# Router of a mixture of experts on unscaled rows, partly inside the product before it

## The reference

```python
def rms_norm(x, g):
    xf = x.astype(jnp.float32)
    y = xf * lax.rsqrt(jnp.mean(xf * xf, axis=-1, keepdims=True) + RMS_EPS)
    return (y * g.astype(jnp.float32)).astype(x.dtype)
...
    g_logits = (xf @ w_rg).astype(jnp.float32) + b_rg.astype(jnp.float32)      # 4 groups
    g_prob = jax.nn.softmax(g_logits, axis=-1)
    g_idx = jnp.argmax(g_logits, axis=-1)
    g_gate = jnp.take_along_axis(g_prob, g_idx[:, None], axis=1)[:, 0]
    e_logits = ...                                                             # 8 experts of that group
    top_vals, top_idx = lax.top_k(e_logits, MOE_TOPK)                          # top 2
    e_gate = jax.nn.softmax(top_vals, axis=-1) * g_gate[:, None]
    ...
    hdn = jax.nn.silu(xb @ w_gate[e]) * (xb @ w_up[e]); return hdn @ w_down[e]
```

## Time and profile before

| | |
|---|---|
| median of 3 runs | 1922.25 us (1921.8 to 1922.73) |
| the profiled execution | 1922.67 us, span 1920.6 us, mean granted TensorE clock 0.968 |
| busy, share of the span | TensorE 91%, VectorE 37%, ScalarE 34%, GpSimd 35% |
| HBM read | 525.82 MB, 274 GB/s over the span |

### The profile page before, as it was taken

How to read it: one execution, slowest core, us unless ns; L and a number is a source line. 1 busy time by engine, 2 the same in 40 slices (tenths; PEclk the granted TensorE clock), 3 DMA queues, 4 the chain that set the end, 5 groups by cost and what they waited for, 6 DMA issues and landing times.

```text
span 1920.6 us, 27786 instructions
## 1 busy us (share of the span) xinstructions
PE 1749.7 (91%) x9070; PEld 1094.1 (57%) x9070; DVE 710.0 (37%) x1363; ACT 656.6 (34%) x1318; POOL 666.4 (35%) x536
## 2 busy tenths in 40 slices
PE   6999999998799999998769999999987999999997
PEld 5889766787444343343358897667864433443432
DVE  5528576423321221221255285674232212222211
ACT  4565555754111111111145665557441111111110
POOL 6688655796000000000056886557950000000000
PEclk9999899998899999999989998999988999999999
DMA  6444211455699999999924442114557999999995
GB/s 254 169 176 174 91 45 45 176 221 218 279 421 426 428 427 428 428 428 427 395 97 158 176 176 89 45 45 176 233 205 291 427 428 427 427 429 427 428 427 251
DMA packets 39770, 528.87 MB, mean 275 GB/s; under 512 B 4248, under 2 KB 7064, under 8 KB 7872
## 3 DMA queue, kind: packets, MB, share of 16 engines
q1 hardware_dynamic: 39584, 526.89, 66.7%
q0 software_dynamic: 32, 0.02, 0.0%
HBM read 525.82 MB, written 1.06 MB: 274 GB/s over the span
## 4 chain that ended last, share of the span: by engine, by line
PE 49%; issue 32%; POOL 8%; DMA 5%; DVE 4%; ACT 1%; SPq 0%; POOLq 0%; DVEq 0%; ACTq 0%
PE PS L1038 9%; POOL view L1946 8%; PE PS L721 5%; PE PS L723 5%; PE PS L722 5%; PE PS L1069 5%; DMA view<-in_w_exp_up_dram 5%; PE PS L855 2%; PE PS L815 2%; PE PS L816 2%; PE PS L817 2%; DVE view L1588 2%; PE PS L1019 2%; PE PS L890 1%; PE PS L1004 1%
## 5 line engine op out<-in xcount | busy, mean ns | idle before, releaser
L1946 POOL TENSOR_TENSOR view<-view,view 128x512 fp32r<-128x512 f32 x448 | 578.6, 1314 | 650.1 <-ACT view L1158 645.3
L1038 PE MATMUL PS<-view,view 128*64 128x512 f32 x2048 | 447.7, 593 | 26.7 <-DMA view<-in_w_exp_up_dram 18.1
L1158 ACT ACTIVATE view<-view 128x512 fp32r<-128x512 f32 x448 | 273.6, 628 | 201.0 <-PE PS L723 189.8
L1038 PEld LDWEIGHTS PS<-view,view 128*64 128x64 f32 x2048 | 146.8, 137 | 321.5 <-issue 321.4
L721 PE MATMUL PS<-view,view 128*128 128x512 f32 x704 | 296.3, 421 | 8.9 <-POOL view L1946 7.2
L723 PE MATMUL PS<-view,view 128*128 128x512 f32 x704 | 276.0, 392 | 0.0
L722 PE MATMUL PS<-view,view 128*128 128x512 f32 x704 | 275.8, 392 | 0.0
L1069 PE MATMUL PS<-view,view 128*64 128x512 f32 x1024 | 231.9, 606 | 1.0 <-ACT view L1407 1.0
L1839 DVE TENSOR_TENSOR view<-PS,view 128x512 f32<-128x512 f32 x32 | 22.1, 692 | 486.7 <-PE PS L1019 421.3
L721 PEld LDWEIGHTS PS<-view,view 128*128 128x128 f32 x704 | 133.6, 190 | 47.4 <-POOL view L1946 12.6
L722 PEld LDWEIGHTS PS<-view,view 128*128 128x128 f32 x704 | 133.6, 190 | 32.8 <-issue 8.2
(11 more groups left out here) (241 smaller groups left out, 2055.8 us busy)
## 6 DMA issues: line engine op xcount, KB each, us to landing
view<-in_w_exp_gate_dram SPq DMA_DIRECT2D x64, 2048.0 KB, 19.9
view<-in_w_exp_up_dram SPq DMA_DIRECT2D x64, 2048.0 KB, 22.7
view<-in_w_exp_down_dram SPq DMA_DIRECT2D x64, 2048.0 KB, 25.8
view<-in_w_mix_dram SPq DMA_DIRECT2D x56, 2048.0 KB, 8.0
view<-bias_table SPq DMA_DIRECT2D x2, 1536.0 KB, 11.4
view<-in_x_dram SPq DMA_DIRECT2D x1, 1024.0 KB, 5.2
out_dram<-view SPq DMA_DIRECT2D x1, 1024.0 KB, 5.3
dtw<-in_w_dt_dram SPq DMA_DIRECT2D x2, 256.0 KB, 11.0
```

The lines of the kernel that those rows point to most:

```text
L1038: ins = pe.matmul(bank(ph, name, j)[e * CAP:(e + 1) * CAP, :], xgT2[h % 2][:, k, at + e * CAP:at + (e + 1) * CAP], slot8[expert_block(j, k ...
L1158: nc.scalar.activation(highs(chunk), weights(slot8, chunk), ACT.Copy).then_inc(*high_ready.up(ph))
L1946: g_.tensor_tensor(weights(low8, chunk), weights(slot8, chunk), highs(chunk), ALU.subtract).then_inc(*low_ready.up(ph))
```

## The change

The transposes and the logits work on `X` itself, before the row factor 1/sqrt is known; the factor (one number for each token) is applied where the bias is added. So the transposes of `X` for blocks 0 to 3 and the logits of blocks 0 to 3 are put behind chunks of the product `("wo", 1)`. The logits are now made transposed, 36 rows by 256 tokens in 8 f32 products (`lgT`), copied out by ScalarE, and turned back by two small products with the identity. `XNh` is made from `X` with the factor as scale (ScalarE), `XNl` by VectorE instead of GpSimd. Mask, `tris` and `ones` for the ranks are bf16. The gate exponentials and the gates move behind the selection of the first four experts, and ranks count from 1 (`iota` starts at 1), which drops one operation. The last two early weight loads wait for `lgT` instead of `lg`.

```diff
-                sp.wait_ge(*full(ph, "lg"))
+                sp.wait_ge(*full(ph, "lgT"))
...
-                product(ph, both("wo", 1), FB + 12, 1, mgTh, mgTl)
-
-                pe.wait_ge(*xn_ready.at(ph, 4))
-                for k in range(KD):
-                    transpose2(ph, lambda t: XN[:, t, k * P:(k + 1) * P], ("h2", k))
-                for k in range(KD - 2, KD):
+                def row_transposes(k):
+
+                    for t in range(TT):
+                        pe.wait_ge(*out_of(ph, "wo", k // 4, t))
+                    transpose2(ph, lambda t: X[:, t, k * P:(k + 1) * P], ("h2", k))
+
+                def logits(k):
+
+                    if k == 0:
+                        pe.wait_ge(*free(ph, "lgT"))
                     pe.wait_ge(*out_of(ph, "h2", k))
+                    return pe.matmul(bank(ph, "lgT")[0:36, 0:TT * P], wr[:, k, :], hT[:, k, :],
+                                     start=(k == 0), stop=(k == KD - 1))
+
+                def first_rows(k):
+
+                    if 1 <= k <= 4:
+                        row_transposes(k - 1)
+                    elif k in (5, 6):
+                        for i in (2 * (k - 5), 2 * (k - 5) + 1):
+                            logits(i)
+
+                product(ph, both("wo", 1), FB + 12, 1, mgTh, mgTl, behind=first_rows)
+                for k in range(KD // 2, KD):
+                    row_transposes(k)
+                for k in range(KD // 2, KD):
+                    ins = logits(k)
+                ins.then_inc(*fill(ph, "lgT"))
+                pe.wait_ge(*out_of(ph, "lgT"))
                 pe.wait_ge(*free(ph, "lg"))
                 for t in range(TT):
-                    for k in range(KD):
-                        ins = pe.matmul(PS[:, 0, t * 36:(t + 1) * 36], hT[:, k, t * P:(t + 1) * P], wr[:, k, :],
-                                        start=(k == 0), stop=(k == KD - 1))
+                    ins = pe.matmul(PS[:, 0, t * 36:(t + 1) * 36], lgs[:, t * P:(t + 1) * P], ident[0:36, 0:36],
+                                    start=True, stop=True)
...
                         act.wait_ge(*out_of(ph, "wo", n, t))
+                        nc.scalar.activation(sq[:, (2 * n + t) * COLS:(2 * n + t + 1) * COLS],
+                                             X[:, t, n * COLS:(n + 1) * COLS], ACT.Square,
+                                             accum_out=small[:, 2 * n + t:2 * n + t + 1]).then_inc(*sumsq.up(ph))
+                    for k in ((4, 6, 7) if n else (0, 2)):
+                        scaled(ph, hT[:, k, :], ("h2", k), G2 + k)
+                act.wait_ge(*full(ph, "lgT"))
+                nc.scalar.activation(lgs, bank(ph, "lgT")[0:36, 0:TT * P], ACT.Copy).then_inc(*drain(ph, "lgT"))
+                act.wait_ge(*r_ready.at(ph, 1))
+                act.wait_ge(*sumsq.made(ph))
                 for t in range(TT):
...
+                    ins = nc.scalar.activation(XNh[:, t, :], X[:, t, :], ACT.Copy, scale=st[:, 64 + t:65 + t])
+                ins.then_inc(*xnh_ready.up(ph))
...
-                norm_rows(8, 15, 4)
-                for k in range(1, KD, 2):
-                    scaled(hT[:, k, :], ("h2", k), G2 + k)
-
+                    for k in ((5,) if n else (1, 3)):
+                        scaled(hT[:, k, :], ("h2", k), G2 + k)
+                dve.wait_ge(*sumsq.at(ph, 17))
+                link(v.tensor_tensor(st[:, 0:TT], small[:, 0:TT], small[:, TT:2 * TT], ALU.add))
+                r_row = rsqrt(TT, 8, D, r_ready)
...
+                for t in range(TT):
+                    ins = v.scalar_tensor_tensor(out=logit[:, t, :], in0=PS[:, 0, t * 36:(t + 1) * 36],
+                                                 scalar=r_row[:, t:t + 1], in1=bc_rb, op0=ALU.mult, op1=ALU.add)
+                ins.then_inc(*drain(ph, "lg"))
...
+                link(v.scalar_tensor_tensor(out=rt[:, 3], in0=rt[:, 2], scalar=-3.0 * BIG, in1=l32,
+                                            op0=ALU.mult, op1=ALU.add))
                 first_max(rt[:, 3], v2, rt[:, 4], rt[:, 5], EXPERTS)
...
+                v.tensor_tensor(maskh[:, :, :], rt[:, 2], rt[:, 5], ALU.add).then_inc(*mask_ready.up(ph))
+                dve.wait_ge(*xnh_ready.at(ph, 1))
+                for t in range(TT):
+                    ins = v.scalar_tensor_tensor(out=XNl[:, t, :], in0=X[:, t, :], scalar=r_row[:, t:t + 1],
+                                                 in1=XNh[:, t, :], op0=ALU.mult, op1=ALU.subtract)
+                ins.then_inc(*xnl_ready.up(ph))
                 dve.wait_ge(*full(ph, "rank"))
...
                 select(0)
-                for i in (1, 3):
-                    gathered_out(0, i)
+                v.tensor_tensor(rs4[:, 0], gl, wide(gmax, GROUPS), ALU.subtract).then_inc(*soft.up(ph))
+                v.tensor_tensor(dd, v2, v1, ALU.subtract).then_inc(*soft.up(ph))
+                v.tensor_reduce(cmax[:, :], PS[:, 1, 64:96], AX, ALU.max).then_inc(*drain(ph, "rank"))
+                dve.wait_ge(*out_of(ph, "rank"))
+                v.tensor_scalar(flag[:, :], cmax[:, :], float(CAP), None, ALU.is_gt).then_inc(*flag_ready.up(ph))
+                gathered_out(0, 1)
+                dve.wait_ge(*rexp.at(ph, 1))
+                gates()
+                gathered_out(0, 3)
+                weigh(0)
```

More of the change, by code:

```diff
@@ L160, in mixer_fills @@
     f += [(("h2", k), 4 + k % 4) for k in range(KD)]
-    f += [(("lg",), 0), (("rank",), 1)]
+    f += [(("lgT",), 2), (("lg",), 0), (("rank",), 1)]
     f += [(("xg", 0, i), b) for i, b in enumerate((7, 2, 5, 6))]
@@ L1450, in link, with rsqrt @@
                     dve.wait_ge(*dve_step.made(ph))
-                def rsqrt(n, count, width):
+                def rsqrt(n, count, width, done=None):
                     var, half, y, a, r = (st[:, o:o + n] for o in (0, 16, 32, 48, 64))
@@ L1462, in rsqrt @@
                         link(v.scalar_tensor_tensor(out=a, in0=a, scalar=-0.5, in1=var, op0=ALU.mult, op1=ALU.mult))
-                        link(v.scalar_tensor_tensor(out=r if step == 2 else y, in0=a, scalar=1.5, in1=y,
-                                                    op0=ALU.add, op1=ALU.mult))
+                        ins = v.scalar_tensor_tensor(out=r if step == 2 else y, in0=a, scalar=1.5, in1=y,
+                                                     op0=ALU.add, op1=ALU.mult)
+                        if step == 2 and done:
+                            ins.then_inc(*done.up(ph))
+                            dve.wait_ge(*done.made(ph))
+                        else:
+                            link(ins)
                     return r
@@ L1708, in layer @@
                 dve.wait_ge(*full(ph, "lg"))
-                v.tensor_tensor(logit, PS[:, 0, 0:72].rearrange("p (t e) -> p t e", t=TT),
-                                bc_rb.unsqueeze(1).to_broadcast([P, TT, 36]), ALU.add
-                                ).then_inc(*drain(ph, "lg"))
+                for t in range(TT):
+                    ins = v.scalar_tensor_tensor(out=logit[:, t, :], in0=PS[:, 0, t * 36:(t + 1) * 36],
+                                                 scalar=r_row[:, t:t + 1], in1=bc_rb, op0=ALU.mult, op1=ALU.add)
+                ins.then_inc(*drain(ph, "lg"))
                 dve.wait_ge(*out_of(ph, "lg"))
@@ L1750, in layer @@
-                link(v.tensor_tensor(gw[:, :, :], gw[:, :, :], rt[:, 1], ALU.add))
-                dve.wait_ge(*full(ph, "rank"))
-                link(v.scalar_tensor_tensor(out=rt[:, 7], in0=PS[:, 1, 0:64].rearrange("p (t e) -> p t e", t=TT),
-                                            scalar=1.0, in1=rt[:, 6], op0=ALU.add, op1=ALU.mult))
-                link(v.tensor_scalar(rk[:, :, :], rt[:, 7], -1.0, None, ALU.add))
-                v.tensor_reduce(cmax[:, :], PS[:, 1, 64:96], AX, ALU.max).then_inc(*drain(ph, "rank"))
@@ L1757, in layer @@
-                dve.wait_ge(*out_of(ph, "rank"))
-                v.tensor_scalar(flag[:, :], cmax[:, :], float(CAP), None, ALU.is_gt).then_inc(*flag_ready.up(ph))
+                v.tensor_tensor(maskh[:, :, :], rt[:, 2], rt[:, 5], ALU.add).then_inc(*mask_ready.up(ph))
[3 more added lines that the diff above has]
+                                                 in1=XNh[:, t, :], op0=ALU.mult, op1=ALU.subtract)
@@ new lines, in layer, with gates @@
+                ins.then_inc(*xnl_ready.up(ph))
+                dve.wait_ge(*full(ph, "rank"))
+                dve.wait_ge(*mask_ready.at(ph, 1))
+                link(v.scalar_tensor_tensor(out=rk[:, :, :], in0=PS[:, 1, 0:64].rearrange("p (t e) -> p t e", t=TT),
+                                            scalar=1.0, in1=maskh[:, :, :], op0=ALU.add, op1=ALU.mult))
+                def gates():
+                    link(v.tensor_reduce(gsum, rs4[:, 1], AX, ALU.add))
+                    link(v.reciprocal(ggate, gsum))
+                    dve.wait_ge(*rexp.at(ph, 2))
+                    link(v.tensor_scalar(w1, ee, 1.0, None, ALU.add))
+                    link(v.reciprocal(w1, w1))
```

(9 more changed lines are left out.)

55 lines of the change are left out of this document (21 added, 34 removed).

## The result

The changed kernel takes 1904.18 us (median of 6 runs, 1903.0 to 1908.98) against 1922.03 (6 runs, 1917.93 to 1923.25): ratio 0.9918, 95% interval 0.9906 to 0.993. That is 17.9 us less; 23.0 were forecast. The profiled execution took 1903.0 us, its span is 1901.3, the mean granted clock 0.978. The sign and most of the part in front of the experts came as predicted; the size did not, and the experiments look for the missing 5.1 us. The median lies outside the forecast's own range, 1896.5 to 1901.5, and inside the wider one, 1895 to 1905.

The account below looks back on a forecast made before the run. Bound: a chain of handovers up to the end of g(0), pair 0's gate product, where the weight stream starts. 2.9 + 13.65 + 8.0 = 24.55 against 36.06 us, 11.5 a layer, 23.0 for two: 1899.3, range 1896.5 to 1901.5.

Parts of the forecast that it names:

- the forecast's own range: Whole kernel: 1896.5 to 1901.5 us, from the bounds on product and gather; chance 0.68.
- the wider one: Whole kernel: 1895 to 1905 us, the range that leaves out no more than 0.2.
- Bound, and what sets g(0): Weight stream starts at the end of g(0), pair 0's gate product; a chain of handovers, 36.06 us in layer 2, precedes it.
- rival (d): Expert weight loads: the stream's bytes, not its start, set the end, so no change, 1922; chance 0.03.
- The product: `("wo", 1)` gets longer by the transposes and logits put inside it: 2.9 us a layer, bounds 1.9 to 3.1.
- The transposes' term: Inside `("wo", 1)`: four pairs of transposes behind chunks add 0.25 us each, 1.0 together.
- rival (e): Inside `("wo", 1)`: TensorE stalls waiting for ScalarE, making the kernel slower, 1927 at a 10 us stall; chance 0.03.
- rival (c): Shorter still: logit records at 0.21 us or a gather wholly at full clock, 1895 to 1897; chance 0.08.
- E' to the logits, picking, `XNl`, gather, g(0): From the lengthened product's end (E'): logits at 5.1 us, mask 10.05, `XNl` 2.4, gather 13.65, g(0) 8.0 after gather's start.
- rival (b): `XNl` pays a port price on VectorE: 1907 at half the price, 1916 at the whole; chance 0.04.
- Rival (a): The clock falls before the last logits behind the product: 2.1 us a layer, 1903.5; chance 0.14.
- delay of 0.74: Gather to g(0): nine gate operations between drains make VectorE reach `xg` 3 0.74 us late, with only g(0) queued behind.

Follow-up runs that it names:

- c3: Changed kernel with three edits: gates behind the drain of `xg` 3, first logits behind the product, `lambda` behind the first transposes; 1896.4 us, ratio 0.988.
- e2: Kernel before with twenty tiny linked VectorE operations between the drains of `xg` 1 and `xg` 3; 1931.39 us, one execution.
- b1: Changed kernel with the four logit products moved out of the product `("wo", 1)`, transposes left in it; 1900.35 us, ratio 0.9892.
- b2: Changed kernel with tile 0 of `XNl` made by GpSimd, tile 1 by VectorE; 1906.76 us, ratio 0.9926.
- b3: Changed kernel with mask, strict triangle and ones for the ranks in f32 as before; 1906.22 us, one run.
- a2: Changed kernel with all eight transposes and all eight logit products behind the product instead of inside it; 1905.44 us, ratio 0.992.
- e1: Kernel before with ten tiny linked VectorE operations between the drains of `xg` 1 and `xg` 3; 1924.62 us, one execution.
- e4: Changed kernel with gates late, first logits behind the product, `lambda` late, plus twenty tiny linked operations between the two drains; 1907.47 us, one execution.
- a3: Changed kernel with the nine gate operations behind VectorE's drain of `xg` 3 instead of before it; 1902.08 us, ratio 0.9903.
- a6: Changed kernel with the gates behind the drain of `xg` 3, profiled once more; 1899.68 us, single run.
- d1: Kernel before with twelve tiny ScalarE copies added to each layer in the router; 1920.41 us, one run.

## Why the prediction was wrong, point by point

*Bound, and what sets g(0)*: right. The layer's end moved with g(0), but for the falls behind it; rival (d) is out (c3's and e2's tails moved the end, down and up).

*The product*: 2.9 predicted, with bounds 1.9 to 3.1, and 3.41 measured in every layer of the changed kernel. The transposes' term was right, 1.0 and 1.00; the logits' was too small, four products and two switches at 1.9 for 2.41 (b1 against the changed kernel). A logit product took 0.48 us in a row of its own kind (0.43 predicted, worked out from 13.73 us for 64 records where rows 4 have 13.96) and 0.6 between chunks. That is 0.5 us a layer, hidden in the time from the start to E' (+3.2 and +2.8), because the stretches ahead of the product came out shorter. No stall, so rival (e) is out; the logits came at 0.48 and not at 0.21, and the clock was 0.51 up to the gather, so rival (c) is out.

*E' to the logits, picking, `XNl`, gather, g(0)*: logit operations at E'+5.27 (5.1), gather at E'+13.76 (13.65), g(0) 7.96 behind it (8.0), g(0)'s end at E'+28.8 (28.7). `XNl` 2.47 (2.4): rival (b) is out while GpSimd rests, and b2 shows what it costs when it doesn't. In f32 the rank products would not be quite hidden (b3, 0.3 us a layer). Rival (a) is out: 1.00 until 472, with four pairs of transposes in between; the rule of the Trainium skill that transposes do not count as busy ("TensorE: Matmul & The Clock Gate", Part 4: PE-mode transpose) does not show in these rows. In a2, where TensorE waits 1.85 us ahead of the remaining transposes, the clock did fall before the logits in layer 1, and did not in layer 2.

*The step that failed* is this one: "Everything behind g(0) is the same in both kernels; it moves with g(0), microsecond for microsecond". Behind g(0) the changed kernel lost 3.6 us. Two things broke it.

First, the clock at pair 0. The gates between the drains were priced at their delay of 0.74 us, behind which only g(0) is queued. The delay was right (g(0) 7.96 us behind the gather's start, 8.0 predicted). But the clock was taken as unchanged there, and the longer idle time costs it: five falls in three of the six layers profiled of the changed kernel, three in the down product, 1.4 to 1.7 us each, and two in g(0) itself, 1.7 each. The three make 1.5 us an execution behind g(0), the two 1.1 in front of its end. That more idle time makes it fall is shown by e1, e2 and e4, and that it stays up with less by a3, a6 and c3; at the length it has here, 1.8 to 2.1 us, it falls in some layers and not in others. The range of the sum had a term for the clock only ahead of g(0).

Second, the next layer does not start like the one before: 1.7 us at the boundary, by a longer standstill of ScalarE, which puts GpSimd's work on top of VectorE's (1.0 us in one operation), and by a slightly later start of VectorE (0.4). That the standstill hangs on what stands in ScalarE's list is shown (d1); how the list sets it is open, beyond the instruction packet named above.

The missing 5.1 us then are: 1.0 in the product, 1.3 from E' to g(0)'s end (1.1 of it the falls in g(0)), 1.9 in the two expert stages (1.5 of it the falls in the down product), 1.7 at the boundary, less 0.8 by which the stretches ahead of the product happened to be shorter. That last part is luck, and so is that the median lies in the wider range of 1895 to 1905: this range was drawn for rivals (a) and (c), and neither came.

What stays open: why the clock falls at 1.79 to 1.88 us of idle time and not at 1.93 and 2.01; and the other falls in the expert stage, which come in the kernel before too (a down product of 9.41 us at 773 us) and whose cost no run isolates. Without a fall at pair 0, g(0) to the layer's end differs by up to 2 us between executions.

Where did the gain come from? From in front of the logits alone: 18.7 to 4.1 us behind E' (7.7 to 9.3 without the hooks), less the 3.4 by which the product is longer. Behind the logits the changed kernel is no faster (24.7 us where the clock holds in g(0), 25.3 on the mean, against 24.4): what the detours gave, copy, turning back and `XNl` took. The unscaled rows with the transposed logits are worth 9 to 11 us a layer in front of the logits (a2), the placement in the product 0.2, or 1.9 where the clock would fall without it, bf16 0.3; the gates between the drains cost 0.4 to 0.9 and the falls.

## What to carry to other kernels

Work slipped between two drains that TensorE waits for costs its delay and, if TensorE then idles longer than it did, perhaps the clock for the next few microseconds: read the granted clock of the rows behind a changed wait, not only the wait. A factor on rows can go behind a product that is linear in them, and takes a norm off the path. Look for TensorE's waits ahead of you before filling a busy product: two of the four products in a wait of 0.9 us and two at the end (b1) beat the same four between chunks by 1.5 us a layer. And in a loop, look at the seam to the next turn as a stage of its own.

## What the hardware showed unexpectedly

- Twelve more tiny operations in ScalarE's list (d1) lengthened its standstill at the start of layer 2 from 5.6 to 5.8 us to 7.25, in a place some 470 us behind them. Ten or twenty more in VectorE's (e1, e2, e4) shortened VectorE's from 8.8 to 9.4 us to 6.6 to 6.9.
- In d1's tail the clock rose from low to high at the end of the transposes or in the wait of 0.66 us behind them, and fell again while TensorE was doing f32 logits (1.00 from 472.4 to 475.0, 0.55 in the next microsecond); the logits were ready 2.4 and 2.9 us earlier. Layer 1 of e2 did the same, and the two profiles of the kernel before did not.
- GpSimd's one operation of 2.34 us held a VectorE operation of 0.22 us for 2.13 (b2).
